# A hybrid decoder layer on one core: first loads from arrays of their own, the first expert pass in a new order, two refills in pieces

## What is computed

```python
proj = x @ p['w_in']                      # q | k | v | rnn-x | rnn-y | gates
o_attn = window_attention(...)            # window 128, ALiBi, sinks
y_rnn  = rglru_branch(...) * gelu(yr)
merged = sigmoid(ga) * (o_attn @ w_attn_out) + sigmoid(gb) * (y_rnn @ w_rnn_out)
x = layer_norm(alpha * x + merged @ w_out)
# mixture of experts, top 4 of 32
logits = x @ w_router + b_router
gate = softmax(top4(logits))
h = x_e @ w_up[e] + b_up[e]               # per expert, 1024 -> 2 x 1024
glu = minimum(h[:, :1024], 7); lin = clip(h[:, 1024:], -7, 7)
y_e = (glu * sigmoid(1.702 * glu) * (lin + 1)) @ w_down[e] + b_down[e]
x = layer_norm(alpha * x + sum_e gate_e * y_e)
```

## Time and profile before

| | us |
|---|---|
| median of 3 runs | 1244.42 |
| lowest, highest | 1244.26, 1245.05 |
| profiled execution | 1246.15 |
| its span | 1244.3 |
| mean granted TensorE clock in it | 0.995 |

### The profile page before, as it was taken

One profiled execution on the slowest core, in us unless ns is written; L12 is line 12 of the kernel. 1 busy time (PEld: TensorE's weight loads), 2 busy tenths in 40 slices (PEclk: granted clock), 3 DMA queues, 4 the chain that ended last, 5 costly groups with the idle time before them and its releaser, 6 DMA issues.

```text
span 1244.3 us, 14964 instructions
## 1 busy us (share of the span) xinstructions
PE 1207.3 (97%) x6445; PEld 585.0 (47%) x6445; DVE 373.7 (30%) x844; ACT 195.8 (16%) x421; POOL 4.6 (0%) x12
## 2 busy tenths in 40 slices
PE   8999999999899999999999999999999999999996
PEld 7888888877333333333333333333333333333332
DVE  0567156135322222222222223222222222222223
ACT  1244473000111010001111100101011010000002
POOL 0000000000000000000000000000000000000000
PEclk9999999999999999999999999999999999999998
DMA  9632454972899999999999999999999999999994
GB/s 371 216 115 98 150 220 161 326 278 83 355 379 428 429 431 429 431 431 430 430 430 429 431 431 430 430 429 432 431 429 430 430 428 432 430 430 431 429 432 164
DMA packets 55121, 451.99 MB, mean 363 GB/s; under 512 B 5760, under 2 KB 24384, under 8 KB 27640
## 3 DMA queue, kind: packets, MB, share of 16 engines
q1 hardware_dynamic: 54352, 448.59, 87.0%
q10 hardware_dynamic: 432, 1.08, 0.3%
q0 software_dynamic: 272, 1.37, 0.3%
HBM read 449.69 MB, written 2.45 MB: 363 GB/s over the span
## 4 chain that ended last, share of the span: by engine, by line
PE 75%; DMA 23%; DVE 1%; issue 0%; ACT 0%; SPq 0%; DVEq 0%
PE pair L1148 24%; DMA slots<-in_w_up 16%; PE pair L1185 14%; PE pair L920 13%; DMA raw<-in_w_up 7%; PE pair L984 5%; PE pair L1099 3%; PE pair L1213 3%; PE pair L1005 2%; PE pair L1176 1%; PE pair L1113 1%; PE pair L1136 1%; PE pair L1128 1%; DMA raw<-in_w_tiled 1%; PE pair L915 1%; PE pair L868 1%
## 5 line engine op out<-in xcount | busy, mean ns | idle before, releaser
L1148 PE MATMUL pair<-slots,xg 128*64 128x512 f32 x1424 | 321.8, 598 | 12.3 <-DMA slots<-in_w_up 11.9
L1148 PEld LDWEIGHTS pair<-slots,xg 128*64 128x64 f32 x1424 | 99.0, 137 | 214.7 <-issue 189.3
L1658 DVE TENSOR_TENSOR xT<-xT,pair 128x528 f32<-128x528 f32 x120 | 76.5, 699 | 395.2 <-PE pair L1213 395.2
L1185 PE MATMUL pair<-slots,at 128*64 128x512 f32 x736 | 167.9, 598 | 0.8 <-ACT at L786 0.8
L920 PE MATMUL pair<-xT,raw 128*128 128x264 f32 x704 | 159.6, 386 | 0.0
L1148 PE MATMUL pair<-raw,xg 128*64 128x512 f32 x624 | 141.1, 595 | 5.8 <-DMA raw<-in_w_up 5.8
L920 PEld LDWEIGHTS pair<-xT,raw 128*128 128x128 f32 x704 | 132.7, 190 | 22.7 <-issue 0.4
L782 ACT ACTIVATE sig<-gsb 128x512 f32<-128x512 f32 x32 | 20.1, 629 | 468.4 <-DVE gsb L1668 468.4
L1185 PEld LDWEIGHTS pair<-slots,at 128*64 128x64 f32 x736 | 48.9, 136 | 92.5 <-issue 80.3
L1148 PEld LDWEIGHTS pair<-raw,xg 128*64 128x64 f32 x624 | 43.1, 137 | 94.4 <-issue 80.2
L1213 PE MATMUL pair<-gt,ysb 64*128 64x264 f32 x496 | 69.5, 409 | 0.0
(11 more groups left out here) (284 smaller groups left out, 819.2 us busy)
## 6 DMA issues: line engine op xcount, KB each, us to landing
slots<-in_w_up SPq DMA_DIRECT2D x89, 2048.0 KB, 28.9
slots<-in_w_down SPq DMA_DIRECT2D x46, 2048.0 KB, 33.4
raw<-in_w_up SPq DMA_DIRECT2D x39, 2048.0 KB, 35.0
raw<-in_w_down SPq DMA_DIRECT2D x18, 2048.0 KB, 36.8
raw<-in_w_tiled SPq DMA_DIRECT2D x22, 1024.0 KB, 5.1
raw<-in_w_rnn_out SPq DMA_DIRECT2D x8, 640.0 KB, 11.5
raw<-in_w_attn_out SPq DMA_DIRECT2D x4, 1024.0 KB, 5.1
raw<-in_w_out SPq DMA_DIRECT2D x4, 1024.0 KB, 4.9
```

The costliest lines, as they stand in the source:

```text
L1148: last = pe.matmul(to[h * CAP:(h + 1) * CAP, :], xg[:, 2 * (i % 2) + row, i // 2, :], w[:, c:c + 512], start=False, stop=i == UPP - 1 and ...
L1185: last = pe.matmul(DOWN[h * CAP:(h + 1) * CAP, :], at[:, kk, i - UPP, :], w[:, kk * D + h * 512:kk * D + (h + 1) * 512], start=i == UPP an ...
L1658: ins = dve.tensor_tensor(y, y, more, ALU.add)
```

## The change

1. The three first pieces of the tokens and of the first weight chunk are input arrays of their own, each contiguous, in place of slices.
2. ACT computes the three exponentials before it takes the first gathered tokens. DVE computes the softmax right after the one-hot of tile 1, first for the sample tile, then for both prompt tiles in one go, and copies the columns after that.
3. `turn_routes` stands ahead of `up(0)`, in place of a `stay_busy(3)`, and writes the banks ACTT and DOWN. `routes` for block 0 follows `up(1)`, ahead of `up_end`. DVE makes the one-hot of block 1 before it takes the routes of block 0.
4. Refill 10 is loaded in two halves: the first when PE is through with the first half of pair 0 (`half_used`), the second when it is through with all of it.
5. The last pair is loaded in three pieces, and `down` waits for each where it needs it.

The core of the diff (waits and copies that only change their bank left out):

```diff
+LAST_PARTS = ((0, 2), (2, 3), (3, 4))
 # SP
-    sp.dma_start(slot(c)[:, k0 * 256:k1 * 256], a["w_tiled"][at0, :, k0 * 256:k1 * 256])\
-        .then_inc(done, 16)
+    sp.dma_start(slot(c)[:, k0 * 256:k1 * 256], a[f"w_first{i}"]).then_inc(done, 16)
...
+    if q == NP:
+        dst, src = refill_parts(Blk(b, None, False), i, b * D)
+        sp.wait_ge(half_used, 1)
+        sp.dma_start(dst[:, 0:2, :], src[:, 0:2, :]).then_inc(first_refill, 16)
+        sp.wait_ge(used_up, 1)
+        sp.dma_start(dst[:, 2:4, :], src[:, 2:4, :]).then_inc(place(Blk(b, None, False), i)[1], 16)
+        continue
...
+    if i == PER - 1:
+        dst, src = refill_parts(Blk(NSTAT, n, True), i, (NE - 1) * D)
+        for (k0, k1), done in zip(LAST_PARTS, last_part):
+            sp.dma_start(dst[:, k0:k1, :], src[:, k0:k1, :]).then_inc(done, 16)
 # ACT
-    act.dma_start(xT[:, k0:k1, :], a["xT"][:, k0:k1, :]).then_inc(s_xT[i], 16)
+    act.dma_start(xT[:, k0:k1, :], a[f"xT{i}"]).then_inc(s_xT[i], 16)
...
     turned_x1(3, 5)
+    for i, t in enumerate(ORDER):
+        exponentials(t, i + 1)
...
     take_turned(Blk(0, None, False))
-    for i, t in enumerate(ORDER):
-        exponentials(t, i + 1)
 # PE
-    pe.wait_ge(gates_ready, 1)
-    for i, to in ((2, GATH), (5, TURN)):
+    pe.wait_ge(gates_ready, 2)
+    for i, to in ((2, ACTT), (5, DOWN)):
...
+def first_routes():
+    pe.wait_ge(routes_copied, 5)
+    routes()
...
+    if blk.first == 0 and i == 0 and row == 0:
+        last.then_inc(half_used, 1)
...
+    if blk.first == 1 and i == NP - PER:
+        pe.wait_ge(first_refill, 16)
     for kk in range(4):
+        if final and kk in [k0 for k0, _ in LAST_PARTS]:
+            pe.wait_ge(last_part[[k0 for k0, _ in LAST_PARTS].index(kk)], 16)
...
     up_end(blk)
-    if blk.first == 0:
-        pe.wait_ge(routes_copied, 5)
-        routes()
-    else:
+    if blk.first > 0:
         pe.wait_ge(added, count(blk, 4, 0))
...
     turn_gathered(begin)
-    stay_busy(3)
-    run(begin, turn_routes)
+    turn_routes()
+    run(begin, first_routes)
 # DVE
     dve.tensor_scalar(onehot[:, 1, :], iota, R(2, 1)[:, 0:1], None, ALU.is_equal).then_inc(onehot_ready, 1)
+    dve.wait_ge(mask_ready, 3)
+    softmax(rows_of(2), slice(2, 3), 3).then_inc(gates_ready, 1)
+    softmax(slice(0, P), slice(0, 2), 3).then_inc(gates_ready, 1)
...
-    for t in ORDER:
-        softmax(t)
-    dve.sem_inc(gates_ready, 1)
...
+    dve.wait_ge(gathered, 1)
+    one_hot(1)
+    dve.wait_ge(spread, 1)
+    select_rows(1)
     take_routes(begin, 0)
     copy_gates(begin)
-    next_rows(begin, 1)
     activate(begin)
 # the inputs
+    pieces = {}
+    for i, (k0, k1) in enumerate(FIRST):
+        pieces[f"xT{i}"] = turned[:, k0:k1]
+        pieces[f"w_first{i}"] = w_tiled[D // 256, :, k0:k1].reshape(P, -1)
```

More of the change, by code:

```diff
@@ L375, in build @@
         ln2_loaded = sem("ln2_loaded")
+        half_used = sem("half_used")
+        first_refill = sem("first_refill")
+        last_part = [sem(f"last_part{i}") for i in range(len(LAST_PARTS))]
         v = sem("v")
@@ L496, in expert_pair, with refill_parts @@
                              src.rearrange("(p k) n -> p k n", p=P)).then_inc(landed, 16)
+            def refill_parts(blk, i, row0):
+                dst, _, _ = place(blk, i)
+                return (dst.rearrange("p (k n) -> p k n", k=4),
+                        w_down[bass.ds(row0 + (i - UPP) * 4 * P, 4 * P), :].rearrange("(p k) n -> p k n", p=P))
             for c, (kind, at0) in enumerate(chunks):
@@ L503, in _ @@
                     if c == 0:
-                        for (k0, k1), done in zip(FIRST, first_part):
-                            sp.dma_start(slot(c)[:, k0 * 256:k1 * 256], a["w_tiled"][at0, :, k0 * 256:k1 * 256])\
-                                .then_inc(done, 16)
+                        for i, ((k0, k1), done) in enumerate(zip(FIRST, first_part)):
+                            sp.dma_start(slot(c)[:, k0 * 256:k1 * 256], a[f"w_first{i}"]).then_inc(done, 16)
                         n0 = FIRST[-1][0] * 256
-                    pieces = [(slot(c)[:, n0:], a["w_tiled"][at0, :, n0:])]
+                    pieces = [(slot(c)[:, n0:], a[f"w_first{len(FIRST) - 1}"] if c == 0 else a["w_tiled"][at0])]
                 elif kind in ("wa", "wx"):
@@ L558, in _ @@
                         continue
-                    if q >= NP:
+                    if q > NP:
                         sp.wait_ge(used_up, q - NP + 1)
-                    elif q >= NP - RING // 2:
+                    elif NP > q >= NP - RING // 2:
                         c = NCH - RING + 2 * (q - (NP - RING // 2))
@@ L585, in _ @@
                     sp.wait_ge(used_up, n * PER + ((NSTAT - 1) * PER + q - LOOP_PAIR - NP + 1))
-                expert_pair(Blk(NSTAT, n, True), i, (NE - 1) * D)
+                if i == PER - 1:
+                    dst, src = refill_parts(Blk(NSTAT, n, True), i, (NE - 1) * D)
+                    for (k0, k1), done in zip(LAST_PARTS, last_part):
+                        sp.dma_start(dst[:, k0:k1, :], src[:, k0:k1, :]).then_inc(done, 16)
+                else:
+                    expert_pair(Blk(NSTAT, n, True), i, (NE - 1) * D)
             sp.wait_ge(used_up, n * PER + ((NSTAT - 1) * PER + LN2_PAIR + 1))
@@ L1179, in down @@
             def down(blk, i):
-                landed(blk, i)
                 w, _, _ = place(blk, i)
+                final = blk.last and i == PER - 1
+                if not final:
+                    landed(blk, i)
+                if blk.first == 1 and i == NP - PER:
+                    pe.wait_ge(first_refill, 16)
                 for kk in range(4):
+                    if final and kk in [k0 for k0, _ in LAST_PARTS]:
+                        pe.wait_ge(last_part[[k0 for k0, _ in LAST_PARTS].index(kk)], 16)
                     for h in range(2):
@@ L1562, in select, with softmax @@
                 dve.tensor_scalar(rsm[r, 0, t:t + 1], m8[r, t, 0:1], -1.0, None, ALU.mult).then_inc(top_ready, 1)
[L1564 to L1572, removed]
+            def softmax(r, t, value):
+                n = t.stop - t.start
+                dve.wait_ge(exp_ready, value)
+                e, total = rt[r, 5, t, :], rsm[r, 2, t]
+                link(dve.tensor_tensor(e, e, rt[r, 4, t, :], ALU.mult))
+                link(dve.tensor_reduce(total, e, AX.X, ALU.add))
+                link(dve.reciprocal(rsm[r, 3, t], total))
+                return dve.tensor_tensor(e, e, rsm[r, 3, t].unsqueeze(2).broadcast_to([r.stop - r.start, n, NE]), ALU.mult)
             chunk_ready(dve, CH_LN)
@@ L1689, in _ @@
             dve.wait_ge(routes_turned, 1)
-            dve.tensor_copy(bx[96:128, 0:T], GATH[0:NE, 0:T]).then_inc(routes_copied, 1)
-            dve.tensor_copy(bx[96:128, 512:512 + T], TURN[0:NE, 0:T]).then_inc(routes_copied, 1)
-            dve.tensor_copy(posmT, GATH[0:NE, 0:T]).then_inc(routes_copied, 1)
+            dve.tensor_copy(bx[96:128, 0:T], ACTT[0:NE, 0:T]).then_inc(routes_copied, 1)
+            dve.tensor_copy(bx[96:128, 512:512 + T], DOWN[0:NE, 0:T]).then_inc(routes_copied, 1)
+            dve.tensor_copy(posmT, ACTT[0:NE, 0:T]).then_inc(routes_copied, 1)
             for h in range(2):
-                dve.tensor_copy(gateT[h * NE:(h + 1) * NE, :], TURN[0:NE, 0:T]).then_inc(routes_copied, 1)
+                dve.tensor_copy(gateT[h * NE:(h + 1) * NE, :], DOWN[0:NE, 0:T]).then_inc(routes_copied, 1)
+            dve.wait_ge(gathered, 1)
+            one_hot(1)
+            dve.wait_ge(spread, 1)
+            select_rows(1)
             take_routes(begin, 0)
             copy_gates(begin)
-            next_rows(begin, 1)
             activate(begin)
@@ L1804, in layouts @@
         sinks[h::32, 0] = x["attn_sinks"][0, h]
-    return {"xT": tokens.T.reshape(KD, P, T).transpose(1, 0, 2),
+    turned = tokens.T.reshape(KD, P, T).transpose(1, 0, 2)
+    w_tiled = x["w_in"][0].reshape(KD, P, PROJ // 256, 256).transpose(2, 1, 0, 3)
+    pieces = {}
+    for i, (k0, k1) in enumerate(FIRST):
+        pieces[f"xT{i}"] = turned[:, k0:k1]
+        pieces[f"w_first{i}"] = w_tiled[D // 256, :, k0:k1].reshape(P, -1)
+    return {**pieces,
             "kcT": x["cache_k"][0].reshape(DECB, WIN, KVW).transpose(2, 0, 1),
-            "w_tiled": x["w_in"][0].reshape(KD, P, PROJ // 256, 256).transpose(2, 1, 0, 3).reshape(-1, P, KD * 256),
+            "w_tiled": w_tiled.reshape(-1, P, KD * 256),
             "small": np.concatenate([vectors.T, by_feature(states).reshape(P, RT * 32), sinks], 1),
```

## The result

The changed kernel takes 1238.38 us in the median of 5 runs (1237.77 to 1239.12), the kernel before 1244.31 (1244.2 to 1245.05): a ratio of 0.9948, 95% interval 0.9936 to 0.9959. I had forecast 1240.8 and a range from 1238.6, so the gain of 5.9 us is larger than the 3.6 I gave it, and lies outside.

A forecast was written before the change was run, and what follows sets the result against it. The full-rate stream of expert weights was taken as the bound, after an early part set by PE. Gains of 3.2 us (stream) and 0.4 (first pieces), 3.6 together, off the median 1244.42 gave 1240.8 us, range 1238.6 to 1243.3.

The forecast's parts named there:

- The limit: Expert weight stream at 430 GB/s: its last not-full moment, plus bytes left at that rate, plus a fixed tail, sets the time.
- The new order: First pass reordered: down(4) starts 4.1 us earlier, the weight stream gains 3.2 us, bounds 2.3 to 4.0.
- The waits: PE's first-pass waits for the one-hot (1.72 us) and the activation (1.63) disappear, 3.35 us together.
- the turned routes under cover: Turning the routes before up(0) replaces six filler matmuls and covers ACT's copy of xg, costing only 0.1 us.
- the gates in time: DVE's softmax gives the gates at 318.2 us, before PE needs them at 319.1: a slack of 0.9 us.
- the closed hole: Stream hole from 344.5 to 350 us, 2.6 us lost before refill 14, shrinks to a loss of 0.3 at most.
- The half refill given back: Refill 10's first half goes out at 322.0 for 323.68, but the third refill waits for pair 2: no gain by itself.
- the last pair free: Splitting the last weight pair into three pieces changes nothing, since the last down doesn't wait for it: zero either way.
- The first pieces: Contiguous first loads at the kernel's start gain between 0 and 2.3 us; 0.4 taken.
- the row it is nearest to: A contiguous refill after idle, 172 GB/s at 324 to 326 us, leaves 0.8 to 1.1 us for the layout.
- rival A: First pieces at the start come at full rate: 2.3 us in place of 0.4, so 1238.9 us; chance 0.13.
- The lower clock: Rival: PE drops to 1.2 GHz in the first pass after waiting for late gates; whole pass about 1252 us; chance 0.05.

The follow-up runs named there:

- the padded variants: The kernel before with first pieces as arrays of their own, rows padded to the old pitch or to 10496 bytes: 1243.98 and 1242.93 us.
- the fillers: The kernel before with filler matmuls (twelve and eight) in PE's two first-pass waits, with the first pieces as own arrays and without: 1242.79 and 1245.86 us.

## Why the prediction was wrong, point by point

- *The limit.* Right. The span is the stream's position plus 927.7 to 929.1 us in all 17 traces.
- *The new order.* Right in size and place: 3.2 forecast, 3.1 to 3.7 measured alone. (Between the profiles of before and after the stream gained 4.2, over the forecast's bound of 4.0.) The waits, the turned routes under cover, the gates in time and the closed hole all came as worked out; `down(4)` gained 4.5 us after `up(0)` where I said 4.1.
- *The half refill given back, the last pair free.* Right, 0 and 0.
- *The first pieces.* Here it failed. The term was 0.4 us and is 3.2 between the two profiles, 2.8 in the median of the traces. The step was "the row it is nearest to": I set the slow start beside a contiguous refill that also starts slowly after idle, and put 1.2 to 1.5 of the 2.3 us lost down to a cold start that no layout can mend. The runs show that the start is not of that kind: with contiguous pieces the DMA engines move 407 GB/s from 3 to 4 us and 403 to 461 from then to 8, where before they moved 179 and 196 from 3 to 5. The likeness was in the symptom, not the cause, and the difference that I named myself under rival A, narrow rows out of wide ones, was nearly it: the padded variants show that the pitch of the wide rows counts, 279 GB/s at 8192 bytes and 369 at 10496. Rival A (1238.9, chance 0.13) is what happened in the main; its page's rule I set aside since its cases began at 512 KiB, which was no evidence about 8 KiB. Even A's 2.3 was short of 3.2, because the bound itself was wrong: it counted bytes below full rate, and what passes through is PE's waits, 3.14 us in before, which are all gone. From 2 to 8 us the stream won only 1.5 us worth of bytes (376 for 268 GB/s), but the bytes it had lost were those of the pieces: the third piece of the chunk lands 6.6 us after its issue where it took 10.2, the last tokens 7.0 where they took 10.1.
- *The lower clock.* Given as a rival of 0.05 for the kernel after, and not seen from 320 to 343 in it. But it came ahead of `up(0)`, where I hadn't looked: in the profiled execution of the change (0.50 from 310 to 312) and in the one of before that my working read (0.57 from 312 to 316), which was 1.7 us longer than the median. The 0.90 of the earlier trace rows, from 304.75 to 321.20, is this stretch. Of before's 28 runs beside the single parts, eight took over 1245.5 us and half under 1244.6; of the 29 beside the fillers, four took over 1249. So it isn't the usual case, and not a rare one. I took the gain off the median, so this cost the forecast nothing.
- *The range.* It began 0.2 us above the result. Rival A, given more weight, would have carried it lower.

What stays open: why the low stretch of the clock falls into the routing in some executions of one kernel and not in others, and why the pieces alone have a mean clock of 0.994 or less in seven of their 11 runs where before has it in two of the 28 beside them.

## What to carry to other kernels

When a stage is bound by a stream that nothing throttles any more, find the last moment at which the stream was not full; only what moves that moment counts, and one rate over one window gave the span of every variant here to within 1.4 us. A gain at the start is bounded by the waits it removes, not by the bytes below full rate. A slow start of loads may be their row pitch: change the pitch alone before calling it a cold start. And a gain at the front can be hidden by the PE clock falling somewhere behind it, so read the spread of runs with their clocks, not the median alone.

## What was not expected of the hardware

- A row pitch of 8192 bytes with rows of 2 and 4 KB held the loads from 2 to 8 us at 261 to 282 GB/s in all traces that have it; with a pitch of 10496 bytes it was 369, contiguous 367 to 387.
- The granted clock fell to its lower level (1.2 of 2.4 GHz) with PE busy for all of it (0.50 from 312 to 316 us, 4.00 of 4.00 us busy, behind small matmuls of routing and norm), in six of 17 traces, and in other executions of the same code it didn't. It put `up(0)` 1.56 or 3.05 us late, with no value between.
- In the pieces alone, 1.72 us of waiting with small work around it was followed by 0.56 and 0.59 over 8 us, and with the half refill alone by 0.80 and 0.50, while the kernel before had the same wait at a full clock.
